# First weights issued from ScalarE's queue and split by VectorE; the last block's variance and the shares of its output pieces rearranged

## The reference

```python
def rmsnorm(x, g):
    x32 = x.astype(jnp.float32)
    y = x32 * lax.rsqrt(jnp.mean(x32 * x32, axis=-1, keepdims=True) + RMS_EPS)
    return (y * g.astype(jnp.float32)).astype(x.dtype)
...
    hn = rmsnorm(h, mix_norm_g[i])
    proj = h @ w_in                       # the first matmul of the program
...
        out = jnp.einsum('bsd,de->bse', merged, w_out[l])
        x = x + _rmsnorm(out, norm_post_w[l])
```

## Time and profile before

| what | value |
|---|---|
| median of 3 runs | 2136.1 us (2135.9 to 2136.1) |
| the profiled execution's own time | 2136.04 us |
| its span in the trace | 2134.4 us |
| granted TensorE clock, mean | 0.999 |
| PE busy | 2124.9 us (100% of the span) |
| DVE busy | 1410.9 us (66%) |
| ACT busy | 1048.7 us (49%) |
| POOL busy | 61.7 us (3%) |
| HBM read | 390.87 MB, 184 GB/s over the span |
| chain that ended last | PE 99% |

### The profile page before, as it was taken

How to read it: one execution, slowest core, us unless ns; L and a number is a source line. 1 busy time by engine, 2 the same in 40 slices (tenths; PEclk the granted TensorE clock), 3 DMA queues, 4 the chain that set the end, 5 groups by cost and what they waited for, 6 DMA issues and landing times.

```text
span 2134.4 us, 34220 instructions
## 1 busy us (share of the span) xinstructions
PE 2124.9 (100%) x12178; PEld 1872.4 (88%) x12178; DVE 1410.9 (66%) x1913; ACT 1048.7 (49%) x1371; POOL 61.7 (3%) x114
## 2 busy tenths in 40 slices
PE   9999999999999999999999999999999999999998
PEld 8888899888888888888888888888888888888886
DVE  7777766666666666645556767867777776566564
ACT  6465665544444444444445555444454454444444
POOL 1001220000000000000000000000000000000000
PEclk9999999999999999999999999999999999999999
DMA  8585334556565565555555455545555455655564
GB/s 301 182 277 190 135 122 158 183 184 194 178 197 190 182 197 178 194 181 202 189 190 178 165 177 188 186 160 188 187 179 177 169 187 182 197 192 184 190 198 147
DMA packets 109317, 396.58 MB, mean 186 GB/s; under 512 B 12386, under 2 KB 12402, under 8 KB 109104
## 3 DMA queue, kind: packets, MB, share of 16 engines
q1 hardware_dynamic: 106848, 386.97, 54.6%
q0 software_dynamic: 2240, 8.38, 1.2%
q10 hardware_dynamic: 144, 0.03, 0.0%
HBM read 390.87 MB, written 2.13 MB: 184 GB/s over the span
## 4 chain that ended last, share of the span: by engine, by line
PE 99%; ACT 0%; DMA 0%; DVE 0%; POOL 0%; issue 0%; DVEq 0%; SPq 0%
PE set L1574 51%; PE set L1582 27%; PE set L1600 4%; PE set L1606 2%; PE set L1548 2%; PE set L1550 2%; PE set L1549 2%; PE misc L1717 1%; PE set L1688 1%; PE set L1534 1%; PE set L1535 1%; PE set L1536 1%; PE misc L1790 1%; PE misc L1777 1%; PE misc L1937 0%; PE set L1692 0%
## 5 line engine op out<-in xcount | busy, mean ns | idle before, releaser
L819 DVE TENSOR_TENSOR w_hl<-raw,w_hl 128x1024 fp32r<-128x1024 f32 x729 | 885.4, 1223 | 556.4 <-ACT w_hl L495 549.7
L495 ACT ACTIVATE w_hl<-raw 128x1024 fp32r<-128x1024 f32 x729 | 762.0, 1056 | 787.8 <-PE set L1582 353.5
L1574 PE MATMUL set<-x_hl,w_hl 128*128 128x512 f32 x3520 | 857.4, 393 | 0.0
L1574 PEld LDWEIGHTS set<-x_hl,w_hl 128*128 128x128 f32 x3520 | 644.5, 188 | 124.3 <-issue 0.7
L1582 PEld LDWEIGHTS set<-x_hl,w_hl 128*128 128x128 f32 x3520 | 452.9, 191 | 18.4 <-issue 0.7
L1582 PE MATMUL set<-x_hl,w_hl 128*128 128x256 f32 x3520 | 462.6, 283 | 0.0
L1574 PE MATMUL set<-f_hl,w_hl 128*128 128x512 f32 x704 | 168.7, 391 | 0.0
L1574 PEld LDWEIGHTS set<-f_hl,w_hl 128*128 128x128 f32 x704 | 129.2, 188 | 24.9
L502 ACT ACTIVATE cross<-set 128x512 f32<-128x512 f32 (+1 forms) x142 | 83.1, 585 | 123.3 <-PE set L1574 111.1
L1582 PEld LDWEIGHTS set<-f_hl,w_hl 128*128 128x128 f32 x704 | 90.8, 191 | 3.7
L1600 PE MATMUL set<-w_hl,x_hl 128*128 128x512 f32 x384 | 92.9, 391 | 0.0
(11 more groups left out here) (324 smaller groups left out, 1802.3 us busy)
## 6 DMA issues: line engine op xcount, KB each, us to landing
raw<-in_weights SPq DMA_DIRECT2D x730, 512.0 KB, 4.0
bias_g<-bias POOLq DMA_DIRECT2D x4, 572.0 KB, 3.3
cur<-in_cur POOLq DMA_DIRECT2D x4, 535.0 KB, 3.6
h<-in_x SPq DMA_DIRECT2D x4, 512.0 KB, 6.9
bias<-u_dram POOLq DMA_DIRECT2D x1, 2048.0 KB, 14.6
out<-y_t SPq DMA_DIRECT2D x8, 256.0 KB, 2.1
post_row<-in_post POOLq DMA_DIRECT2D x1, 1024.0 KB, 6.5
w<-in_w POOLq DMA_DIRECT2D x1, 256.0 KB, 5.2
```

Source lines behind the costliest of these rows:

```text
L495: a(high, whole, ACT.Copy).then_inc(hi_ready, 1)
L819: tt(low, whole, high.bitcast(F32), ALU.subtract).then_inc(lo_ready, 1)
L1574: last = mm(out[:, f * 2 * S:(f + 1) * 2 * S], w[:, 0, c], hl[:, kt, :, :], start=first and k == 0, stop=low_first, skip_group_check=True)
```

## The change

- SP no longer loads chunk 0. ACT issues that load on its own queue, right behind the gains.
- ACT no longer makes the high part of the first half of chunk 0. DVE does, with `tensor_copy`, as its first step, which waits for chunk 0. DVE's low parts of x's blocks 0 and 1 come behind it.
- In the last block DVE's `splits` is called with count NB - RING = 4, and one more `split` follows for chunk 7 of the block. So DVE waits for the fourth chunk and not for the seventh before `post_variance(0)`.
- Of the pieces of t = 1, (1, 2) is now scaled by ACT and added by POOL, and (1, 3) is finished by DVE. ACT's scaling no longer waits for `out_taken` at 8. SP's order of the pieces is the same, with the two counters exchanged.

```diff
@@ -374,7 +374,6 @@
             sp.dma_start(h[:, 4 * n:4 * n + 4, :], d["x"][:, 4 * n:4 * n + 4, :]).then_inc(x_in[n], 16)
 
         load_x(0)
-        load(0, 0)
         load(1, 1)
         load(2, 2)
         load_x(1)
@@ -393,7 +392,7 @@
             sp.wait_ge(lo_ready, c - RING + 1)
             load(c, c % RING)
         for t, q, ready, count in ((0, 0, y_ready, 1), (0, 1, y_ready, 2), (0, 2, y2_ready, 1), (0, 3, y2_ready, 2),
-                                   (1, 0, y_ready, 3), (1, 1, y_ready, 4), (1, 2, y_ready, 5), (1, 3, y2_ready, 3)):
+                                   (1, 0, y_ready, 3), (1, 1, y_ready, 4), (1, 2, y2_ready, 3), (1, 3, y_ready, 5)):
             sp.wait_ge(ready, count)
             sp.dma_start(piece(d["out"], t, q), piece(y_t, t, q)).then_inc(y_out, 16)
         sp.wait_ge(y_out, 8 * 16)
@@ -474,7 +473,7 @@
 
         pool.wait_ge(chunks_done, C_WO)
         pool.dma_start(post_row[:, :], bass.AP(tensor=d["post"].tensor, offset=0, ap=[[0, P], [1, D]])).then_inc(post_in, 16)
-        for n, (t, q) in enumerate(((0, 2), (0, 3), (1, 3))):
+        for n, (t, q) in enumerate(((0, 2), (0, 3), (1, 2))):
             pool.wait_ge(y_scaled, n + 1)
             g.tensor_tensor(piece(y_t, t, q), piece(y_t, t, q), h_t[:, t, q - 2, :], ALU.add).then_inc(y2_ready, 1)
 
@@ -528,6 +527,8 @@
             return a(dst, src, ACT.Square, scale=scale)
 
         act.dma_start(gains[:, :, :], d["gains"]).then_inc(gains_in, 16)
+
+        act.dma_start(raw[0][:, :], d["weights"][0]).then_inc(raw_ready[0], 16)
         def operands(n):
             act.wait_ge(x_in[n], 16)
             for kt in range(4 * n, 4 * n + 4):
@@ -542,7 +543,6 @@
         operand(bass.ds(0, 1), MIX)
         operand(bass.ds(1, 1), MIX)
         act.wait_ge(raw_ready[0], 16)
-        a(w_hl[0][:, 0, 0:BLK], raw[0][:, 0:BLK], ACT.Copy).then_inc(hi_half, 1)
         operand(bass.ds(2, 1), MIX)
         operand(bass.ds(3, 1), MIX)
         a(w_hl[0][:, 0, BLK:], raw[0][:, BLK:], ACT.Copy).then_inc(hi_ready, 1)
@@ -800,8 +800,7 @@
         square_out(3, 1)
         post_root(1)
         act.wait_ge(post_ready, 2)
-        act.wait_ge(out_taken, 8)
-        scale_out(1, 3)
+        scale_out(1, 2)
 
 
     @block.vector
@@ -863,6 +862,8 @@
                 operand(bass.ds(kt, 1), MIX, kt + 1)
 
         start = Pos(C_KV)
+        dve.wait_ge(raw_ready[0], 16)
+        v.tensor_copy(w_hl[0][:, 0, 0:BLK], raw[0][:, 0:BLK]).then_inc(hi_half, 1)
         dve.wait_ge(gains_in, 16)
         operands(range(0, 2))
         dve.wait_ge(hi_half, 1)
@@ -1490,7 +1491,11 @@
         dve.wait_ge(post_in, 16)
         splits(Pos(C_WO + NB), NB, takes_out(0))
         splits(Pos(C_WO + 2 * NB), NB, takes_out(1))
-        splits(Pos(C_WO + 3 * NB), NB - 1, takes_out(2) | {3: first_squares})
+
+        last_block = Pos(C_WO + 3 * NB)
+        splits(last_block, NB - RING, takes_out(2) | {3: first_squares})
+        for j in range(NB - RING, NB - AHEAD):
+            split(last_block, j + AHEAD)
         post_variance(0)
         take_out(3, 0)
 
@@ -1506,7 +1511,7 @@
         finish(1, 0, m[2][:, :])
         finish(1, 1, m[3][:, :])
         dve.wait_ge(ht_taken, 2)
-        finish(1, 2, h_t[:, 1, 0, :])
+        finish(1, 3, h_t[:, 1, 1, :])
 
 
     @block.tensor
```

## The result

The changed kernel takes 2138.87 us (median of 22 runs, 2137.45 to 2139.3) against 2136.05 for the kernel before (22 runs, 2135.9 to 2136.22): a ratio of 1.0013 with a 95% interval of 1.0007 to 1.0018. That is 2.8 us slower, which is within the 0.2% that the prediction called no change, but outside its range. The profiled execution took 2138.84 us, its span is 2137.2.

A forecast was written before the change was run, and what follows sets the result against it. TensorE, 99% of the chain, was taken as the bound, so only the two ends count: start +1.95 us and end -1.35 sum to +0.6, giving 2136.7 us beside the median of 2136.1, range 2134.7 to 2138.2.

The forecast's parts named there:

- What bounds it: Whole kernel: TensorE is 99% of the chain, so a delay of chunk 0 moves every later matmul by the same amount.
- Start, step 1, the landing: Program start: chunk 0 on ACT's queue takes turns with chunk 1 and lands at 7.7 instead of 6.08 us.
- Step 2, from the landing to chunk 1: Start: with DVE's CAST (0.47) ahead of its low parts, landing to chunk 1's first matmul takes 4.34 us, 0.33 longer.
- The clock: Rival at the start: idle TensorE falls to its lower clock, costing 1.3 to 2.6 us; time 2138.7, chance 0.1.
- The range: Whole kernel: time between 2134.7 and 2138.2 us.
- the clock's milder case: Start: the clock stays low for 2.6 us, half of it lost, costing 1.3 us; rival's chance 0.1.
- The end: After the last matmul: earlier square, shorter third finish and earlier last piece give -1.35 us, bounds -0.9 and -1.6.
- the square: End: ACT's square of t = 1 starts 0.03 after the last matmul, at 2126.41 instead of 2126.92, -0.51 us.
- the third finish: End: DVE's third finish overlaps POOL's add for only 0.29 us and ends at 2130.45 instead of 2131.29, -0.84.
- the last issue: End: SP issues the last piece at 2130.48, -1.22 us, since piece (1, 2) is ready ahead of it.
- the landing of the last piece: End: the last piece, sent alone, takes 2.0 to 2.2 us to land instead of 2.3, -0.15.

The follow-up runs named there:

- the run with nothing behind x: Changed kernel, but SP waits for chunk 0's landing before issuing chunk 1 and all behind it; chunk 0 stays on ACT's queue: 2136.79 us.
- the run with more warm-up: Changed kernel with 21 warm-up matmuls instead of 14: 2137.66 us.
- the pieces alone: Kernel before with only the pieces of t = 1 exchanged between POOL and DVE and ACT's wait for out_taken at 8 dropped: 2135.73 us.
- the end change alone: Changed kernel with its start as before (SP loads chunk 0, ACT makes the first high half): 2135.24 us against 2136.18 for the kernel before.

## Why the prediction was wrong

- **What bounds it** was right: the shift of the start, 3.8 us, arrived whole at the last matmul.
- **Start, step 1, the landing.** The mechanism was right, two queues in turn, and the Trainium skill's rule that an engine drains a whole packet of one queue first ("DMA: Bandwidth & Descriptors", "Queues, rings and completion order") is not what the trace shows: 84 against 77 packets in the same stretch, and in the kernel before 27 of x against 24 of the gains from 2.8 to 3.2 us, where a whole packet of x first would have put the gains at the end. The page's other statement ("Issuing engines are not separate DMA queues"), that issuing from several engines saves only issue time, fits: none was saved, as both chunks were issued at 1.32. The loss of 2.1 us comes beside it. The size was off: 8.2, not 7.7. I let both chunks be through at 7.95, and took the earlier of the two for chunk 0, with no row for it. It was the later one: it stood behind the gains, and it shared with chunk 2 as well, since SP's queue had moved 1.18 MB by 7.0 us, 0.13 more than x's quarter and chunk 1. That is +2.1 instead of +1.6. Of the 2.1, 0.6 are not explained by the turns (the run with nothing behind x).
- **Step 2, from the landing to chunk 1,** was right at a full clock: 4.32 measured against 4.34, CAST 0.43 against 0.47.
- **The clock** is the step that failed: the sum holds nothing for it. I made it a rival with a chance of 0.1, deciding "from a landing of about 8.4 on", because at the end of the trace the clock fell 2.6 us after the last matmul and the gap here would be 1.9. The runs showed two things in its place. That 2.6 is no constant: in the profiles of these kernels the clock fell 2.1 to 5.2 us after the last matmul of the program (in that of the pieces alone this ended at 2126.49, and the fall is in the window below, columns of the earlier trace rows). And the fall doesn't need a gap as long as that: in the changed kernel the gap was 2.0 us, and the clock fell 3.0 us after the last warm-up matmul, with TensorE at work again for a microsecond. The fall costs 1.4 us up to chunk 1 (13.91 - 8.2 - 4.34) and 1.2 to 1.4 by the run with more warm-up, where the rival's price was 1.3 to 2.6. In 20 of 22 runs the time is the one with the loss, so one in ten was far too little.

```profile
2131.00:2132.00 1.00, 0.00 (x0) 0.00 (x0) 0.00 (x0) 0.00 (x0) 0.00 (x0) 0.84 1.07 412
```

- **The range.** Its upper end had a late landing without the clock (2138.0). I wrote that it reaches to the clock's milder case too, "or 2138.2 with it", but a late landing with that case is 2138.0 + 1.3 = 2139.3, which would have held the 2138.87. The rival's own time of 2138.7 lay outside the range as well. That it came so near the measured one is in part luck: its price of 2.0 was 0.6 too high, which hid most of the 0.85 that the landing and the end were off.
- **The end** had its steps right: the square -0.5, the third finish 0.85 long, the last issue 4.1 behind the last matmul instead of 5.3. Only the landing of the last piece, which I had 0.15 shorter, was 2.4 us instead of 2.3; the pieces before it are closer now, but no run tests that this is why. -1.0 instead of -1.35.

The sum of the parts: +2.1 (landing) + 0.3 (DVE's order) + 1.4 (clock) - 1.0 (end) = +2.8, as measured.

## What to carry to other kernels

A transfer that was moved to an idle queue was not served sooner here; it gave up its place in line and took turns with all that used to stand behind it. So the first thing that is needed belongs on the same queue as the next ones, ahead of them. Where TensorE's start is made later, its warm-up has to grow with it. Price the gap with the loss of the clock included; at a gap near 2 us these executions went both ways, more often with the loss. Don't take the delay of a fall from one place in one trace: it differed by 3 us between profiles. And take the gap from more than one execution, since the end of the same warm-up moved by 1.3 us. Of two edits at the two ends of a program, neither covers the other, and each is worth a run of its own.

## What the runs showed of the hardware

- Idle stretches of TensorE between warm-up and first real matmul, in the profiled executions: with 1.94, 1.96, 2.23, 2.37 and 2.90 us the granted clock fell to 0.50, with 0.94, 1.23, 1.56 and 1.88 us it didn't. That is one execution each. The fall came 2.3 to 3.9 us after the last warm-up matmul; in three of the five TensorE was already at work again, in two it was not. The low stretch lasted 3.4 us in all five. Of the changed kernel's 22 runs, 20 have the longer time.
- The records of the warm-up matmuls (128 columns, float32, two for each matmul) are 0.42 us long at first and 0.275 later, and the matmuls 0.43 and then 0.22 us apart. The change came between 4.1 us (the end change alone) and 6.8 us (the changed kernel), in both at the first entry of the granted clock in the trace. Before that entry the views read 1.00, which is not to be relied on.
- 32 KB in 128 small packets took 7.2 us to land behind one 512 KB chunk on the same queue and beside another queue's chunks, 4.1 when first in line.
